# A two-block transformer on one core: first norm's chain, gate units as two matmuls per k tile, channel sums on VectorE, a masked quarter of scores left out

## What is computed

```python
def _even_layer(x, norm_g, w_in, b_glu, w_dw, b_dw, ln_g, ln_b, w_pw, b_pw, w_out):
    z = _rmsnorm(x, norm_g) @ w_in
    a_val, a_gt, a_gate, q, k, v, b_gate = _split_cols(z, [...])
    ya = _conformer_conv(a_val + b_glu[:CONV_WIDTH], a_gt + b_glu[CONV_WIDTH:],
                         w_dw, b_dw, ln_g, ln_b, w_pw, b_pw) * jax.nn.silu(a_gate)
    yb = _moba_attention(q.reshape(shp), k.reshape(shp), v.reshape(shp)) * jax.nn.silu(b_gate)
    return jnp.concatenate([ya, yb], axis=-1) @ w_out
```

## Time and profile before

| | |
|---|---|
| median of 3 runs | 2566.94 us (2566.68 to 2567.55) |
| the profiled execution's own time | 2565.47 us |
| its span in the profile | 2563.7 us |
| mean granted TensorE clock | 0.991 |
| busy share: PE, DVE, ACT, POOL | 97%, 63%, 46%, 6% |
| HBM traffic | 164 GB/s over the span |

### The profile page before, as it was taken

One profiled execution on the slowest core, in us unless ns is written; L12 is line 12 of the kernel. 1 busy time (PEld: TensorE's weight loads), 2 busy tenths in 40 slices (PEclk: granted clock), 3 DMA queues, 4 the chain that ended last, 5 costly groups with the idle time before them and its releaser, 6 DMA issues.

```text
span 2563.7 us, 35901 instructions
## 1 busy us (share of the span) xinstructions
PE 2486.2 (97%) x14366; PEld 2175.2 (85%) x14366; DVE 1622.7 (63%) x1941; ACT 1176.6 (46%) x1371; POOL 151.1 (6%) x136
## 2 busy tenths in 40 slices
PE   6999999999889999999999999999999999999998
PEld 6888998898778788988888888888888888888886
DVE  4799755545674776486565545445677557755764
ACT  5433754444464554542345444334655334433333
POOL 0000000000200100000000000000022001210220
PEclk9999999999999999999999999999999999999999
DMA  7565436554424555554026555535455555655553
GB/s 236 165 197 189 142 131 229 150 165 133 144 83 159 157 185 172 170 164 132 1 82 214 187 180 192 164 132 184 160 182 196 192 183 183 196 187 185 186 174 138
DMA packets 341284, 422.91 MB, mean 165 GB/s; under 512 B 14491, under 2 KB 267178, under 8 KB 340394
## 3 DMA queue, kind: packets, MB, share of 16 engines
q1 hardware_dynamic: 338620, 411.66, 49.1%
q0 software_dynamic: 2160, 8.40, 1.0%
q10 hardware_dynamic: 382, 1.11, 0.1%
HBM read 419.05 MB, written 2.10 MB: 164 GB/s over the span
## 4 chain that ended last, share of the span: by engine, by line
PE 94%; DVE 4%; ACT 2%; issue 0%; DMA 0%; ACTq 0%; DVEq 0%
PE ps L678 29%; PE ps L679 15%; PE ps L723 9%; PE ps L725 9%; PE ps L724 9%; PE ps L681 4%; PE ps L682 4%; PE ps L683 4%; PE ps L944 3%; PE ps L754 1%; DVE w_lo L1844 1%; PE ps L912 1%; PE ps L885 1%; PE ps L1141 1%; PE ps L1132 1%; PE ps L901 0%
## 5 line engine op out<-in xcount | busy, mean ns | idle before, releaser
L678 PE MATMUL ps<-h_cat,w_hi 128*128 128x512 f32 x3200 | 1137.0, 400 | 8.2 <-DVE qo L1877 8.0
L679 PE MATMUL ps<-h_cat,w_lo 128*128 128x256 f32 x3200 | 897.7, 281 | 0.0
L1844 DVE TENSOR_TENSOR w_lo<-ring,w_hi 128x2048 fp32r<-128x2048 f32 (+2 forms) x282 | 592.3, 2102 | 278.6 <-ACT w_hi L1221 275.6
L678 PEld LDWEIGHTS ps<-h_cat,w_hi 128*128 128x128 f32 x3200 | 602.2, 188 | 159.1 <-DVE w_lo L1844 6.1
L679 PEld LDWEIGHTS ps<-h_cat,w_lo 128*128 128x128 f32 x3200 | 605.5, 189 | 2.1 <-issue 1.9
L1221 ACT ACTIVATE w_hi<-ring 128x2048 fp32r<-128x2048 f32 (+2 forms) x282 | 495.8, 1759 | 98.9 <-PE ps L725 84.5
L1840 DVE TENSOR_TENSOR w_lo<-ring,w_hi 128x2048 fp32r<-128x2048 f32 (+1 forms) x136 | 303.1, 2232 | 232.0 <-ACT w_hi L1218 231.9
L1218 ACT ACTIVATE w_hi<-ring 128x2048 fp32r<-128x2048 f32 (+1 forms) x136 | 252.7, 1862 | 285.4 <-PE ps L725 263.4
L723 PE MATMUL ps<-w_hi,h_cat 128*128 128x512 f32 x704 | 275.9, 392 | 4.7 <-DVE h_cat L2013 3.0
L725 PE MATMUL ps<-w_hi,h_cat 128*128 128x512 f32 x704 | 274.7, 390 | 0.0
L724 PE MATMUL ps<-w_lo,h_cat 128*128 128x512 f32 x704 | 274.7, 390 | 0.0
(11 more groups left out here) (380 smaller groups left out, 2460.0 us busy)
## 6 DMA issues: line engine op xcount, KB each, us to landing
ring<-in_w_ffn_up SPq DMA_DIRECT2D x44, 2048.0 KB, 8.0
ring<-in_even_w_in SPq DMA_DIRECT2D x28, 2048.0 KB, 8.1
ring<-in_w_mix_in SPq DMA_DIRECT2D x28, 2048.0 KB, 8.3
ring<-in_w_ffn_down SPq DMA_DIRECT2D x16, 2048.0 KB, 8.0
ring<-in_odd_w_in SPq DMA_DIRECT2D x11, 2048.0 KB, 8.3
ring<-in_even_w_out SPq DMA_DIRECT2D x8, 2048.0 KB, 8.1
ring<-in_odd_w_out SPq DMA_DIRECT2D x8, 2048.0 KB, 8.1
ring<-in_w_mix_out SPq DMA_DIRECT2D x8, 2048.0 KB, 8.1
```

Of the source, the lines that this page charges most:

```text
L678: mm(o[:, 0:2 * T], whi[slot][:, k, :], flat(cat[:, k]), start=first, stop=False)
L679: ins = mm(o[:, T:2 * T], wlo[slot][:, k, :], cat[:, k, 0, :], start=False, stop=end)
L1844: tt(wlo[slot][:, 0:g.kt, 0:m], chunk(c % RING, g)[:, :, u0:u0 + m], whi[slot][:, 0:g.kt, 0:m].bitcast(F32), ALU.subtract).then_inc(sem["l ...
```

## The change

It has four parts.

1. **The start.** x comes in four transfers of 64 tokens, of which SP and ACT issue one each for the first 128 tokens, and then one each for the second. All rows of the first table are issued by POOL, the gain's first and counted on its own. The first chunk is loaded in two transfers, one per unit. The hi part of the very first unit is written by POOL, in two halves (`first_hi`), and its lo part by DVE in two halves (`first_rest`), between the first pieces of `h_cat`. PE turns the gain alone first, and the rest of the table behind the first transposes.
2. **Gate units.** `e_gt`, `e_bgate`, `e_agate`, `o_gate0`, `o_gate1` and `g_z` (48 units) are paired now. ACT's drain is a plain copy; DVE's post adds the other half; and the function follows on ACT in place (`gate_function`, counted by `gated`), one step later.
3. **Channel sums.** DVE sums the 8 channel tiles with a reduction over a rearranged view (`channel_sum`), of `conv` at step 9 and of `csq` at step 14, and PE does one matmul with ones instead of eight, at steps 10 and 12.
4. **The masked quarter.** Queries 0 to 127 take no scores with keys 128 to 255, so that a head has one score matmul of 128 columns and one of 256 instead of two of 256, and p has three transposes instead of four. Those columns of banks 2 and 3 are set to zero once by DVE, at step 0 of `e_bgate`, behind the same `emptied` of 4; PE now waits for that (`quarter_clear`).

```diff
@@ -66,7 +66,8 @@
 
     def __init__(self, name, units, kt, staged=False, wide=False):
         self.name, self.units, self.kt, self.staged, self.wide = name, units, kt, staged, wide
-        self.paired = staged or name in ("e_k", "e_q", "o_iq", "o_q", "g_c", "x_q", "x_k")
+        self.gated = name in ("e_gt", "e_bgate", "e_agate", "o_gate0", "o_gate1", "g_z")
+        self.paired = staged or self.gated or name in ("e_k", "e_q", "o_iq", "o_q", "g_c", "x_q", "x_k")
         self.kq = kt // 4
         self.k0 = 8 if name in ("e_out", "g_out") else 0
         self.per_chunk = 2 if wide else max(2, 2 * KT // kt)
...
+    def gated_tile(g, jj):
+
+        to, first = {"e_gt": (sig, 0), "e_bgate": (bg, 0), "e_agate": (ag, 0), "o_gate0": (gate, 0), "o_gate1": (gate, 8),
+                     "g_z": (gz, 0)}[g.name]
+        return flat(to[:, bass.ds(jj + first, 1), :])
+        if g.name == "e_gt" and isinstance(k, int) and k == 0:
+            return [(slice(u * P, (u + 1) * P), wview(w1, g)[:, :, CW + u * P:CW + (u + 1) * P]) for u in range(2)]
...
-        sp.dma_start(x[:, 0, :], a["x"][0, 0:P]).then_inc(sem["x_loaded0"], 16)
+        for t in range(TT):
+            sp.dma_start(x[0:HALF, t, :], a["x"][0, t * P:t * P + HALF]).then_inc(sem[f"x_loaded{t}"], 16)
...
+        load_rows(pool, first_table[0], "gain_loaded")
+        for row in first_table[1:]:
+            load_rows(pool, row, "params_loaded")
+        pool.wait_ge(sem["first_loaded"], 16)
+        for half in range(2):
+            k = slice(8 * half, 8 * half + 8)
+            pool.tensor_copy(whi[0][:, k, :], chunk(0, order[0])[:, k, 0:P]).then_inc(sem["first_hi"], 1)
...
-        pe.wait_ge(sem["params_loaded"], 16 * len(first_table))
+        pe.wait_ge(sem["gain_loaded"], 16)
+        nc.tensor.transpose(ps[1][:, 0:GAIN], rows[0:GAIN, 0, :], ident[0:GAIN, 0:GAIN]).then_inc(sem["rows_turned"], 1)
+        turn_first(0)
+        pe.wait_ge(sem["params_loaded"], 16 * (len(first_table) - 1))
         turn_rows(0, ps[PRM_BANK]).then_inc(sem["rows_turned"], 1)
-        turn_first(0)
         seg("e_gt", norm=0, also=tables_beside)
...
         def e_scores(h, o):
             for qt in range(TT):
-                ins = mm(o[:, qt * T:(qt + 1) * T], qe[:, h, qt * P:(qt + 1) * P], ke[:, h, :], start=True, stop=True)
+                keys = (qt + 1) * P
+                ins = mm(o[:, qt * T:qt * T + keys], qe[:, h, qt * P:(qt + 1) * P], ke[:, h, 0:keys], start=True, stop=True)
             return ins
...
-                for qt in range(TT):
+                for qt in range(kt, TT):
...
-                    pe.wait_ge(sem["emptied"], 4)
+                    pe.wait_ge(sem["quarter_clear"], 1)
...
                     if h >= 2:
                         pe.wait_ge(sem["o_drained"], h - 1)
                     e_values(h, h).then_inc(sem["o_ready"], 1)
-                if u_ == 11:
-                    pe.wait_ge(sem["conv_tap"], TAPS * CT)
+                if u_ == 10:
+                    pe.wait_ge(sem["conv_total"], 1)
+                    pe.wait_ge(sem["masked"], HEADS - 1)
+                    mm(ps[2][:, 0:T], ones[:], xsq[:], start=True, stop=True).then_inc(sem["conv_mean"], 1)
+                if u_ == 12:
+                    pe.wait_ge(sem["conv_total"], 2)
                     pe.wait_ge(sem["masked"], HEADS)
-                    for c in range(CT):
-                        ins = mm(ps[2][:, 0:T], ones[:], conv[:, c, :], start=(c == 0), stop=(c == CT - 1))
-                    ins.then_inc(sem["conv_mean"], 1)
-                if u_ == 12:
-                    pe.wait_ge(sem["conv_sq"], 1)
-                    for c in range(CT):
-                        ins = mm(ps[3][:, 0:T], ones[:], csq[:, c, :], start=(c == 0), stop=(c == CT - 1))
-                    ins.then_inc(sem["conv_var"], 1)
+                    mm(ps[3][:, 0:T], ones[:], xsq[:], start=True, stop=True).then_inc(sem["conv_var"], 1)
             return also
 
         seg("e_bgate", also=e_heads_beside(0))
...
-        act.dma_start(x[:, 1, :], a["x"][0, P:2 * P]).then_inc(sem["x_loaded1"], 16)
-        for row in first_table:
-            load_rows(act, row, "params_loaded")
-        st = {"split": 0, "drained": 0, "squared": 0}
+        for t in range(TT):
+            act.dma_start(x[HALF:P, t, :], a["x"][0, t * P + HALF:(t + 1) * P]).then_inc(sem[f"x_loaded{t}"], 16)
+        st = {"split": 1, "drained": 0, "squared": 0}
...
+            if g.gated:
+                if g.name == "e_bgate":
+                    act.wait_ge(sem["conv_tap"], 2 * TAPS * (j // 2 + 1))
+                ins = af(gated_tile(g, jj), src, ACT.Copy)
...
+        def gate_function(g, j, i=None):
+
+            jj = j if i is None else j + 4 * i
+            act.wait_ge(sem["summed"], g.d0 + jj + 1)
+            v = gated_tile(g, jj)
+            if g.name == "e_gt":
+                ins = af(v, v, ACT.Sigmoid, bias=col("b_glu", CT + jj))
+            else:
+                ins = af(v, v, ACT.Silu)
+            ins.then_inc(sem["gated"], 1)
+
+        gates_done = {g.name: 0 for g in order if g.gated}
+
+        def functions_to(name, j1):
+            for j in range(gates_done[name], j1):
+                gate_function(S[name], j)
+            gates_done[name] = j1
...
+                if tail is not None and j < 4:
+                    functions_to(tail, max(gates_done[tail], LAG + 2 + j))
+                if g.gated and j > LAG:
+                    functions_to(name, j - LAG)
...
             dve.wait_ge(sem["drained"], g.f0 + jj + 1)
             whole = {"e_k": ke, "e_q": qe, "o_iq": iq, "o_q": qo, "g_c": ysc, "x_q": xq, "x_k": xk}.get(g.name)
             s = g.s0 + j
-            z = stage[:, s % STG, PAD:PAD + T] if g.staged else flat(whole[:, at_j, :])
+            z = stage[:, s % STG, PAD:PAD + T] if g.staged else gated_tile(g, jj) if g.gated else flat(whole[:, at_j, :])
             tt(z, z, bank(g, n)[:, 0:T], ALU.add).then_inc(sem["summed"], 1)
...
+        def first_rest(half):
+
+            k = slice(8 * half, 8 * half + 8)
+            dve.wait_ge(sem["first_hi"], half + 1)
+            tt(wlo[0][:, k, :], chunk(0, order[0])[:, k, 0:P], whi[0][:, k, :].bitcast(F32), ALU.subtract)\
+                .then_inc(sem["lo_ready" if half else "first_lo"], 1)
+
         def turned_rows(k, source):
 
             scaled(k, source, 0)
             scaled(k, source, 1)
             for c in (2, 3):
+                if k == 0:
+                    first_rest(c - 2)
                 lo(k, 2 * c - 4), lo(k, 2 * c - 3)
                 scaled(k, source, c)
             if k == 0:
+                dve.wait_ge(sem["rows_turned"], 2)
+                copy_params(range(1))
                 split_to(2)
...
+        def channel_sum(tiles):
+
+            nc.vector.tensor_reduce(xsq[:], tiles[:].rearrange("p c t -> p t c"), AX_X, ALU.add).then_inc(sem["conv_total"], 1)
+
         def e_heads_beside(u0):
             taps = conv_taps(204, 11)
 
             def also(i, b):
                 u_ = u0 + 4 * i + b
+                if u_ == 0:
+                    dve.wait_ge(sem["emptied"], 4)
+                    for bank_ in (2, 3):
+                        ins = nc.vector.memset(ps[bank_][:, P:T], 0.0)
+                    ins.then_inc(sem["quarter_clear"], 1)
                 if u_ < 4:
                     taps(0, b)
+                if u_ == 9:
+                    dve.wait_ge(sem["conv_tap"], TAPS * CT)
+                    channel_sum(conv)
...
-                    dve.wait_ge(*emptied(S["e_bgate"], h + 1))
+                    dve.wait_ge(sem["gated"], S["e_bgate"].g0 + h + 1)
                 if u_ == 14:
+                    dve.wait_ge(sem["conv_sq"], 1)
+                    channel_sum(csq)
+                if u_ == 13:
                     dve.wait_ge(sem["conv_mean"], 1)
```

More of the change, by code:

```diff
@@ L93, in segments @@
         c += g.chunks
+        g.g0 = gated
+        gated += g.units if g.gated else 0
         paired += g.units if g.paired else 0
@@ L506, in load @@
                 srcs = chunk_src(g, c, 2 * i + b)
-            for cols, src in srcs:
-                sp.dma_start(chunk(slot, g)[:, :, cols], src).then_inc(loaded[slot], 16)
+            for n, (cols, src) in enumerate(srcs):
+                done = sem["first_loaded"] if g is order[0] and not looped and i == b == n == 0 else loaded[slot]
+                sp.dma_start(chunk(slot, g)[:, :, cols], src).then_inc(done, 16)
         for g in order:
```

69 lines of the change are left out of this document (38 added, 31 removed).

## The result

The changed kernel is slower: 2573.70 us in the median of 8 runs (2571.72 to 2575.93) against 2567.24 (2564.23 to 2568.54), a ratio of 1.0027 with a 95% interval of 1.0019 to 1.0036. That is 6.5 us. The prediction had 2568.4 in a range of 2560 to 2574 and "no measurable change" as the likeliest outcome; the time lies in the range, but five us above its value and on the slower side.

The account below looks back on a forecast made before the run. PE was taken as the bound, at 94% of the span. Terms -6.4 -0.7 +5.0 +0.4 +3.9 +1.7 -0.8 -1.6 sum to +1.5 on the median 2566.94, giving 2568.4 us, range 2560 to 2574.

Parts of the forecast that it names:

- A: Whole kernel: the terms as summed, +1.5, own range 2565 to 2572; chance 0.56.
- The start, -6.4: Kernel start: x's first 128 tokens land at 6.2, unit 0 ends at 27.7 to 28.0; -6.4, between -4.4 and -7.7.
- The reduction, 2.2: Step 9 of `e_bgate` to `e_agate`: the sum over `conv` takes 2.2 on DVE and holds up p by 1.8.
- rival B: Channel sums: the strided reduction takes double duration, 4.4; +2.8, 2571.2; chance 0.14.
- Sum of the region: `e_bgate` to `e_agate`: stalls 15.8 and work -10.7 taken as +5.0, plus +0.4 for the clock.
- The wait for `emptied`: `e_bgate`: DVE stands 11.2 before the memsets; PE waits 1.9, 7.1, 0.6 at units 1 to 3, 2.7 at head 0's p.
- Rival C: `e_bgate`: the wait for `emptied` costs PE little; -11.5, 2557, or 2564 with the p stalls alone gone; chance 0.17.
- `o_gate0`, +4.8 in all: Unit 2 of `o_gate0` waits for DVE's post(0): +3.9 of stall, +1.7 for the clock, -0.8 for cheaper units.
- Rival D: `o_gate1` and `g_z`: PE also waits for late posts there; two such stalls make +7, 2575; chance 0.13.
- Pairing, -5.0: The 48 gate units: a paired unit of 16 k tiles saves PE 0.105, 5.0 in all.
- The masked quarter, -2.6: `e_bgate` to `e_agate`: eight heads' scores save 8 x 0.22 and transposes 8 x 0.11, 2.6 of PE's work.
- stalls of 15.8 less 10.7 of work: `e_bgate` to `e_agate`: PE's new waits on DVE 15.8 against PE's work falling by 10.7, summed to +5.0.

Follow-up runs that it names:

- the repairs: The changed kernel with x in two whole transfers, memsets at step 2, sums by three additions and an early post in `o_gate0`: 2550.77 us, ratio 0.9936.

## Why the prediction was wrong

The likeliest case was A, the sum at +1.5 with its own range of 2565 to 2572. Measured is +6.5. That the time still lies in the range says little, since the range was wide enough for rivals on both sides. By its terms:

- **The start, -6.4: this is the step that failed.** The change gave -2.3 there. "With the first 128 tokens in front on both queues, I put their landing half way" took for granted that half transfers move at the rate of whole ones; they moved at 217 to 238 GB/s instead of 353, and the first 128 tokens landed at 8.4 instead of 6.2. x's second half came 4.1 later than before (12.9 against 8.8), and the first half chunk 4.1 later than the 13.0 that I had put. Even the lower bound of this term, -4.4, had the landing as before, and so shut the loss out. The rest of the step holds: with whole transfers in order on one queue the first 128 tokens landed at 6.0 and unit 0 ended 7.1 earlier than before. A smaller error was in it too: a cast on POOL holds DVE up. DVE's half lo part took 2.02 beside the second cast and 1.21 without one, while the two casts took 2.02 together whichever of DVE's instructions stood beside them.
- **The reduction, 2.2: mis-sized.** It took 3.74 and 3.85. The bounds had 4.4 as the doubled price, rival B, which is near. Neighbouring elements went at 0.69 for 512, in a reduction too, so the factor of 1.7 most likely lies in the 1 KB between elements; this reduction also makes 256 sums of 8 where that one makes 2 of 256, and no run here parts the two or tries another distance. The rule of the Trainium skill, SBUF — State Buffer, the note on cachelines, that each access that crosses to a new SBUF line costs, agrees with the rows. B's +2.8 counted only the longer waits, though. What made it worse was the clock: 3.12 us of waiting instead of 1.8 lowered it for 6.1 us, another 3 us, where with 1.77 it stayed up. Sum of the region: predicted +5.4, measured +9.8; by these rows 1.3 of the excess is the longer wait and 3 the clock.
- **The wait for `emptied`: right** in its main steps (11.0 of 11.2; 1.9 and 7.0 at units 1 and 2), and the memsets' move gave back 12.2 where the sum had 11.5. Rival C is thereby out. Its tail came otherwise: the clock cost 1.7 instead of 0.4, no wait stands at unit 3, and p of the first head was waited for 1.43 instead of 2.7. That last wait belongs to pairing, since it outlived the memsets' move (1.40) and was gone without pairing. The sum put it down to the late banks.
- **`o_gate0`, +4.8 in all: right**, +4.7 in the trace, with 4.08 of waiting and about 3.4 us at the lower clock. Rival D did not come: no wait of PE for `gate` or `gz` stands in `o_gate1` or `g_z`, which are 1.6 and 1.1 shorter.
- **Pairing, -5.0: met** as a median difference (4.9), but in part by luck. With the repairs, the traces have 3.0 from the 48 gate units themselves, since they still made PE wait in `e_bgate` and `e_agate`, and 2.6 from `e_val` to `e_q`, which the sum did not touch.
- **The masked quarter, -2.6: no run undoes it alone.** Its rows are as the sum had them: from start to start a head's scores and transposes take 0.65 and 0.33 in the change (at 299.23 and 299.88), 0.86 and 0.44 before (at 286.16 and 287.02).

Two slips of the working change nothing: unit 0 over at 27.7 to 28.0 is 6.0 to 6.3 before 34.0 and not 6.4, and stalls of 15.8 less 10.7 of work are 5.1 and not 5.0.

By the mistakes at the start (4.1) and in the region (4.4) alone, the sum would come out at +10, and the traces of these two executions show +10.2. That agreement is luck. `e_gt` to `e_q` gave 3.3 more than the sum had, `o_gate1` and `g_z` 1.1 more; against that stand 3.0 in `g_qkv` and `g_ab`, 0.9 between `e_pw` and `o_gate0` and 1.2 behind `g_c`.

The medians differ by 6.5 only: the profiled execution of the kernel before lies 1.8 below its median, and that of the change 1.9 above. The 3.0 in `g_qkv` and `g_ab`, which the change does not touch, look like unlike executions rather than the change: a paired k tile of `g_qkv` is short in the traces of the kernel before and of the one where only the channel sums are mended, and long in the other ten, whether gate units are paired or not. The 2.6 in `e_val` to `e_q` look like the change's: these groups are shorter in all ten profiled kernels with paired gate units and in neither of the two without. Why is open. I can't split the 6.5 more finely than that. In the medians whole transfers alone gave back 2.3 and the additions alone 2.7.

## What to carry to other kernels

A transfer that is cut to come earlier must still cover all 128 partitions: cut by rows of work, in order on one queue, not by partitions. When an instruction gets a new wait on an in-order engine, read what is queued behind it and how early it would have stood there; eleven us of standing were repaired by moving two memsets by two steps, and a bank's release by moving one addition. Give a reduction neighbouring elements: halving additions took 2.3 us where the strided form took 3.7. And price a wait of PE with the clock behind it, since one of 3 us cost as much again, and one of 1.8 did not.
